# A fused encoder layer on one core: who issues the transfers of VectorE's turning of x, and when

## The reference

```python
h = rmsnorm(x, g_pre_mix) * (1 + scale1) + shift1
x = x + gate1 * rmsnorm(token_mixer(h, ...), g_post_mix)     # mLSTM heads | 2-D neighbourhood attention
h = rmsnorm(x, g_pre_ffn) * (1 + scale2) + shift2
x = x + gate2 * rmsnorm(expert_choice_moe(h, ...), g_post_ffn)   # 16 experts
```

## Time and profile before

| | us |
|---|---|
| median of 3 runs | 2347.81 (2345.64 to 2349.93) |
| the profiled execution | 2346.43 |
| its span, first to last instruction | 2344.6 |
| TensorE busy | 2238.1 (95%) |
| VectorE busy | 1410.6 (60%) |
| ScalarE busy | 1097.2 (47%) |
| GpSimd busy | 750.6 (32%) |
| mean granted TensorE clock | 0.987 |

### The profile page before, as it was taken

The page is one execution under the profiler, slowest core; times in us unless marked ns, Lnnn a source line. Parts: engine busy times, 40 slices in busy tenths (PEclk is TensorE's granted clock), DMA queues, the critical chain, the costliest instruction groups (busy, mean ns, idle before and its releaser), DMA issues. The chain is left out here.

```text
span 2344.6 us, 34389 instructions
## 1 busy us (share of the span) xinstructions
PE 2238.1 (95%) x13051; PEld 1861.2 (79%) x13051; DVE 1410.6 (60%) x2069; ACT 1097.2 (47%) x1768; POOL 750.6 (32%) x770
## 2 busy tenths in 40 slices
PE   6999999999999999999993999999999999999997
PEld 4679978977899888677772888888888888888886
DVE  3213354555413436665558777777778778888885
ACT  4213442555433435666542445444444445555553
POOL 3003332433233415341003422112222335443534
PEclk9999999999999999999996999999999999999998
DMA  8837785757554449764637576666666679999996
GB/s 317 268 112 231 220 231 170 220 147 190 140 186 153 153 157 245 213 202 142 203 130 273 215 248 229 225 218 225 226 225 228 225 260 310 312 320 322 320 302 230
DMA packets 234878, 524.06 MB, mean 224 GB/s; under 512 B 38964, under 2 KB 138180, under 8 KB 215280
## 3 DMA queue, kind: packets, MB, share of 16 engines
q1 hardware_dynamic: 185360, 407.37, 51.5%
q0 software_dynamic: 49376, 114.78, 17.7%
HBM read 423.71 MB, written 97.88 MB: 222 GB/s over the span
## 5 line engine op out<-in xcount | busy, mean ns | idle before, releaser
L2667 DVE TENSOR_TENSOR moe_w_lo<-moe_wf,moe_w_hi 128x2048 fp32r<-128x2048 f32 x192 | 436.7, 2287 | 196.1 <-ACT moe_w_hi L2523 195.1
L2523 ACT ACTIVATE moe_w_hi<-moe_wf 128x2048 fp32r<-128x2048 f32 x192 | 365.8, 1915 | 376.4 <-PE moe_acc L2853 362.2
L2853 PE MATMUL moe_acc<-moe_w_hi,moe_x_hi 128*128 128x512 f32 x1024 | 398.8, 389 | 0.9 <-DVE moe_x_lo L2673 0.6
L2853 PE MATMUL moe_acc<-moe_w_lo,moe_x_hi 128*128 128x512 f32 x1024 | 398.4, 389 | 0.0
L2853 PE MATMUL moe_acc<-moe_w_hi,moe_x_lo 128*128 128x512 f32 x1024 | 398.4, 389 | 0.0
L2853 PEld LDWEIGHTS moe_acc<-moe_w_hi,moe_x_hi 128*128 128x128 f32 x1024 | 192.2, 188 | 41.4 <-DVE moe_x_lo L2673 0.8
L2853 PEld LDWEIGHTS moe_acc<-moe_w_hi,moe_x_lo 128*128 128x128 f32 x1024 | 192.2, 188 | 40.1
L2853 PEld LDWEIGHTS moe_acc<-moe_w_lo,moe_x_hi 128*128 128x128 f32 x1024 | 192.2, 188 | 39.7
L2397 POOL DMA_INDIRECT moe_xe<-scratch_h,moe_parts x120 | 195.3, 1627 | 87.4 <-issue 76.2
L1874 PE MATMUL banks<-fr_w_hi,fr_h_hi 128*128 128x256 f32 x768 | 222.9, 290 | 0.0
L1874 PE MATMUL banks<-fr_w_lo,fr_h_hi 128*128 128x256 f32 x768 | 217.0, 283 | 0.0
(11 more groups left out here) (322 smaller groups left out, 4374.3 us busy)
## 6 DMA issues: line engine op xcount, KB each, us to landing
moe_wf<-in_w_expert_gate SPq DMA_DIRECT2D x64, 1024.0 KB, 5.7
moe_wf<-in_w_expert_up SPq DMA_DIRECT2D x64, 1024.0 KB, 5.1
moe_wf<-in_w_expert_down SPq DMA_DIRECT2D x64, 1024.0 KB, 6.9
fr_w_raw<-in_w_units SPq DMA_DIRECT2D x28, 1024.0 KB, 6.6
fr_bias<-in_na_bias SPq DMA_DIRECT2D x16, 1520.0 KB, 11.6
fr_a_w<-in_w_ada POOLq DMA_DIRECT2D x16, 1024.0 KB, 8.3
scratch_qk_t<-fr_stage SPq DMA_DIRECT2D x64, 256.0 KB, 2.7
scratch_vov<-fr_stage SPq DMA_DIRECT2D x96, 128.0 KB, 2.3
```

The lines of the kernel that those rows point to most:

```text
L2523: nc.scalar.activation(w_hi[:, q, :, :], wf[:, q, :, :], ACT.Copy).then_inc(w_hi_ready, 1)
L2667: nc.vector.tensor_tensor(w_lo[:, q, :, :], wf[:, q, :, :], w_hi[:, q, :, :].bitcast(F32), ALU.subtract).then_inc(w_lo_ready, 1)
L2853: mm = nc.tensor.matmul(acc[:, j, b, :], x[:, g, k, :], w[:, q, a, h * HALF:(h + 1) * HALF], start=(k == 0 and i == 0), stop=(k == KC - 1 ...
```

## The change

ScalarE issues the 16 loads and 16 stores of the four turning steps in place of SP. Loads are at tick 133 + 12 i, and the store of step i is at tick 145 + 12 i, just before the load of step i + 1; both stand behind `evac` and before `split_w` of their tick. VectorE's turns are at ticks 137 + 12 i and 138 + 12 i. The load of the turned quarter 2 moves from tick 184 to 192, its scaling from 196 to 204, and TensorE's spread of 1/rms for quarter 3 from 208 to 216.

```diff
@@ -165,10 +165,10 @@
 SQ_AT = {2: M1 - 30, 3: M1 - 26}
 TURN_AT = {1: 2 * TICKS + 3, 2: (M1 - 2) * TICKS, 3: (M1 + 2) * TICKS + 1}
 
-XQ_AT, XQ_STEP, XQ_STEPS = M1 - 25, 3, 4
-XT_AT = {2: M1 - 11, 3: M1}
-SPREAD_AT = {2: (M1 - 11) * TICKS, 3: (M1 - 5) * TICKS}
-SCALE_AT = {2: (M1 - 8) * TICKS, 3: (M1 + 2) * TICKS}
+XQ_AT, XQ_STEP, XQ_STEPS = M1 - 24, 3, 4
+XT_AT = {2: M1 - 9, 3: M1}
+SPREAD_AT = {2: (M1 - 11) * TICKS, 3: (M1 - 3) * TICKS}
+SCALE_AT = {2: (M1 - 6) * TICKS, 3: (M1 + 2) * TICKS}
 
 ROWS_AT = [(GATES_AT[g] + 2) * TICKS for g in range(GROUPS)]
 
@@ -501,19 +501,6 @@
                     sp.wait_ge(rows_stored, 64)
                 sp.dma_start(x[:, :, :], x_view[q]).then_inc(x_loaded, 16)
 
-            def load_xq(i):
-                if i:
-                    sp.wait_ge(xq_turned, FIRST_ADA + i)
-                else:
-                    sp.wait_ge(sq_ready, KC * 4)
-                for a in range(4):
-                    sp.dma_start(xa[32 * a:32 * a + 32, :, :], xq_view[XQ_STEPS + i, a]).then_inc(xq_loaded, 16)
-
-            def store_xq(i):
-                sp.wait_ge(xq_turned, FIRST_ADA + i + 1)
-                for a in range(4):
-                    sp.dma_start(xs_view[i, a], xb[32 * a:32 * a + 32, :, :]).then_inc(xq_stored, 16)
-
             def load_xt(q):
                 if q == 2:
                     sp.wait_ge(xq_stored, FIRST_ADA + 64 * XQ_STEPS)
@@ -618,11 +605,6 @@
                                 load_w(LOAD_AT[b])
                             if b in (SQ_AT[2] - 3, SQ_AT[3] - 3):
                                 load_x(2 if b < SQ_AT[2] else 3)
-                            step, late = divmod(b - XQ_AT, XQ_STEP)
-                            if late == 0 and 0 <= step < XQ_STEPS:
-                                load_xq(step)
-                            if late == 2 and 0 <= step < XQ_STEPS:
-                                store_xq(step)
                             if b in XT_AT.values():
                                 load_xt(2 if b < M1 else 3)
                             if b == NBLK - 12:
@@ -1084,6 +1066,19 @@
                     act.drain()
                     nc.scalar.activation(ps[:, PH, :], x[:, j, i * HALF:(i + 1) * HALF], ACT.Square, accum_out=ss[:, j, i:i + 1]).then_inc(sq_ready, 1)
 
+            def load_xq(i):
+                if i:
+                    act.wait_ge(xq_turned, FIRST_ADA + i)
+                else:
+                    act.wait_ge(sq_ready, KC * 4)
+                for a in range(4):
+                    act.dma_start(xa[32 * a:32 * a + 32, :, :], xq_view[XQ_STEPS + i, a]).then_inc(xq_loaded, 16)
+
+            def store_xq(i):
+                act.wait_ge(xq_turned, FIRST_ADA + i + 1)
+                for a in range(4):
+                    act.dma_start(xs_view[i, a], xb[32 * a:32 * a + 32, :, :]).then_inc(xq_stored, 16)
+
             def take_x(k):
                 act.wait_ge(turned, k + 1)
                 nc.scalar.activation(h_raw[:, k, 0:HALF], ps[:, k % 2, :], ACT.Copy).then_inc(xT_ready, 1)
@@ -1190,6 +1185,11 @@
                         if u == 0 and b >= 2:
                             for c in range(0 if b == 2 else b - 1, b):
                                 evac(c)
+                        step, late = divmod(b - XQ_AT, XQ_STEP)
+                        if (late, u) == (0, 1) and 0 < step <= XQ_STEPS:
+                            store_xq(step - 1)
+                        if (late, u) == (0, 1) and 0 <= step < XQ_STEPS:
+                            load_xq(step)
                         for q in (1, 2, 3):
                             if q > 1 and b == SQ_AT[q]:
                                 squares(q, u)
@@ -1552,8 +1552,8 @@
                 for b in range(NBLK):
                     for u in range(TICKS):
                         step, late = divmod(b - XQ_AT - 1, XQ_STEP)
-                        if late == 0 and 0 <= step < XQ_STEPS and u >= 2:
-                            turn_xq(step, u - 2)
+                        if late == 0 and 0 <= step < XQ_STEPS and u in (1, 2):
+                            turn_xq(step, u - 1)
                         for q in (1, 2, 3):
                             if q > 1 and (b, u) == (SQ_AT[q] + 1, 0):
                                 mean_of(q)
```

## The result

The changed kernel takes 2363.41 us (median of 4 runs, 2363.07 to 2366.13) where the kernel before, run beside it, took 2348.77: a ratio of 1.0067, interval 1.005 to 1.0084. It is slower by 0.67%, and the time lies above the forecast of 2351 and its range of 2341 to 2358. The profiled execution took 2363.07 us with a span of 2361.3, against 2346.43 and 2344.6, so its difference of 16.7 us in the span is the one to explain.

The account below looks back on a forecast made before the run. TensorE, busy 95% of the span, was taken as the bound, so only its idle time and clock count. Terms: +3.4 (tick 145, containing tick 133's -1.7) + 0 + 0 + 0 = +3.4 us, giving 2351; range 2341 to 2358.

Parts of the forecast that it names:

- Tick 133: First four loads on ScalarE: issues hidden in its idle time, the 1.73 us gap at qT goes, -1.7 us.
- Tick 145: Eight issues ahead of w_hi delay w_lo and `scores`; TensorE stands 5.0 us: +3.4 with clock, containing the earlier -1.7.
- Tick 157: Eight issues ahead of a weight piece; xa lands just in time for block 41's w_lo: 0, bounds -0.9 and +4.
- My sign for this tick: At tick 157: the forecast is wrong there if a gap over 1.5 us stands before L2072 near 325.
- Tick 169: Issues hide; the 3.78 us gap and 1.5 of clock go, a 3.3 to 5.3 us wait comes at turn_o: 0.
- Tick 181 and the scaling: Last four stores, and scaling moved into the last head's tail: 0, up to +1 for the scaling.
- Rival B: At tick 157, shared rings delay the next head's qT, a gap of 4 to 5 us: 2357 us; chance 0.32.
- Rival A: Issues are cheap on ScalarE, 3.1 us for eight; sum about -6, 2342 us; chance 0.24.

Follow-up runs that it names:

- Experiment 1: The changed kernel with its 32 issues back in SP's queue, at the new ticks; 2369.37 us, ratio 1.0095 against the kernel before.
- experiment 3: The changed kernel with ScalarE's weight piece of a tick ahead of that tick's issues; 2363.89 us, ratio 1.0076 against the kernel before.
- Experiment 5: The changed kernel with VectorE's turns 4 ticks later, from tick 141 + 12 i; 2354.94 us, ratio 1.0031 against the kernel before.
- experiment 7: The kernel before with only the turned x's load, the scaling and quarter 3's spread two blocks later; 2346.24 us, ratio 0.9997.
- experiment 2: The kernel before with ScalarE issuing the 32 transfers, at SP's old ticks; 2344.25 us, ratio 0.9985.
- experiment 10: The kernel before with only the 16 loads on ScalarE, at the old ticks, stores left on SP; 2342.09 us, ratio 0.9984.
- experiment 8: The kernel before, SP issuing, with turns at 137 + 12i and stores at 140 + 12i, ahead of the next load; 2351.44 us, ratio 1.0017.
- experiment 6: The changed kernel with turns 4 ticks later and ScalarE's weight piece ahead of its tick's issues; 2347.11 us, ratio 1.0002 against the kernel before.

## Why the prediction was wrong

**Tick 133: right in its term, with one oversight.** The qT gap went, -1.79 us against -1.7. The sentence that the next state is "due only at 284" took VectorE's wait for hidden. xa landed at 283.37, and the state came 1.18 us late. Experiment 1, with the load issued 5.5 us later still, makes 4.92 us of the same wait.

**Tick 145: right mechanism, undersized.** The chain of issues, w_hi, w_lo and `scores` is what stands in the trace, and experiment 3 takes the gap from 6.56 to 1.70 us by putting w_hi ahead. With the term of tick 133 I had +3.4; it measured +6.9. Eight issues took 7.4 us (3.1 and 4.31), not 6.2, and began later: w_hi started at 301.11 instead of 298.5. The gap was 6.56 us instead of 5.0, and the clock took 2.1 instead of 1.5.

**Tick 157 is the step that failed.** I put 0, with "landing takes 4.0 to 6.0 us" and "it just fits". Landing took 12.6 us behind the last issue. That issue ended 6.9 us later than I put it (331.09 against 324.2), but TensorE asked for block 41 6.7 us later too (339.70 against 333), so this cancels; the landing, 6.6 us over my upper value, and w_lo, 2.24 us against 1.2, make the gap. VectorE stood 9.19 us at the turn, block 41 started 7.43 us late, the clock cost 2.7, and the place measured +9.1 (from +6.87 to +15.96): more than half of the whole loss. Without it the time would have been near 2354, an estimate by the ledger, inside the range. My sign for this tick, a gap over 1.5 us before L2072 near 325, looked at the wrong consumer: there is no gap there, and the 7.43 us stand at block 41.

Two things were wrong in the term. The first is a reading. The 4.0 and 6.0 us are the minimum and median of single transfers, each from its own issue, but the turn waits for the last of four, and I left out the maximum of 9.5 in the same row. The kernel before shows the wait that counts: its first four were issued by 265.89 and the turn started at 273.08, 7.2 us later; its last four were issued by 338.88 and the turn started at 347.75, 8.9 us later.

```profile
273.08 1.25 DVE L1430 STREAM_TRANSPOSE fr_xb<-fr_xa 128x1024 f32<-128x1024 f32 x1 [6.22 <-DMA fr_xa<-in_x]
...
336.03 2.85 SPq L510 DMA_DIRECT2D fr_xa<-in_x  x4
```

With 8.9 the term would have been 324.2 + 8.9 + 1.25 + 1.2 = 335.6, some 2.6 us late and not 0. The second is the place: the rows of the kernel before come from loads at their old places. There the load of tick 152 was issued *ahead* of kT, qT and E, and the one of tick 157 now comes *behind* them, while they are moving. The rows by window say what it met there: the DMA engines' busy share in the changed kernel was 1.03 in 326 to 334 and 0.98 in 334 to 344, against 1.03 and 0.88 in the same windows before. A share near 1 alone does not set the two kernels apart; what differs is which transfers were ahead.

```profile
326.00:334.00 8.00, 8.00 (x45) 6.85 (x44) 1.34 (x3) 2.78 (x5) 2.52 (x2) 1.00 1.03 349
334.00:344.00 10.00, 5.70 (x34) 4.59 (x32) 0.74 (x3) 4.13 (x6) 2.65 (x2) 0.90 0.98 295
```

At the same time the change cut the distance between load and turn: from tick 128 to 134 before, from 133 to 137 now. A tick is some 2.1 us here (24 of them from the score at 302.09 to the one at 353.56), so 12.6 us became 8.4, of which the eight issues take about 7. Experiment 5 gives four ticks back and the turns' waits fall from 29.6 to 8.7 us.

**Tick 169: right.** The 3.78 us gap and its clock went (the ledger falls by 5.45, from +15.96 to +10.51), and 4.53 us with clock stands before turn_o; I had a wait of 3.3 to 5.3 us and a sum of 0, and it measured +0.9 (from +15.96 to +16.86). **Tick 181 and the scaling: right**, 0 by the ledger and by experiment 7.

**Rival B** had the side and nearly the size, but not the place. It let qT come late because two queues share the DMA engines; the gap at qT closed. What came late enough to be waited for was xa. Other transfers of SP did slow down, as it said: at tick 157 the next head's v landed 11.4 us after its issue and the first E 12.9, against 9.1 and 9.0 before. With a single ring, in experiment 1, the third xa landed no sooner after kT's issue (21.2 us against 20.6), so this lateness can come without a second ring; whether the ring shares in it where there are two, no run tells apart. **Rival A** (cheap issues, 3.1 us for eight) is refuted by the 6.8 to 7.4 us that eight took. But its sign was right for the half of the change that it is about: at the old places, experiment 2, ScalarE's issues did pay.

What stays open: whether xa was late because its packets waited behind those of the next head, or because each of those transfers slowed all others. Both give a late landing under load; that at tick 157 even the first of the four landed 11.6 us after its issue fits either. No run here took the next head's loads away. Nor was a kernel run with tick 157 alone at its old place.

## What to carry to other kernels

When a load is moved, take its landing time, that of the last transfer of the group, from what else is in flight at the new place and not from its own rows at the old one, and count the ticks from the load to its consumer again. A consumer that waits in an in-order queue makes everything behind it late, so putting single instructions ahead of it only moves the gap, and two late causes at one place must be taken away together before the gain of either shows there. An issue costs its engine half a microsecond to one: give an idle engine's queue the loads that must start early, and leave stores where nothing waits behind them.

## What the runs showed of the hardware

- The price of an issue depends on what was queued just before. A load issue on ScalarE took 472 ns in the median when it stood alone (322 to 569, experiment 2), and 848 ns in the changed kernel (403 to 1906), where three of the four groups stand right behind four stores. These three groups took 3.54 to 4.31 us for four, the first, without stores ahead, 2.56.
- The same megabyte, in four transfers, landed 5.4 us after its last issue at tick 169 and 12.6 and 13.2 us beside the next head's loads. In experiment 1 the delay lay in SP's queue instead: it began the third four 10 us behind kT, took 5.33 us to issue them, and they landed 5.9 us later (341.73 to 347.65).
- TensorE's clock fell from 2.4 to 1.2 GHz for a part of the time behind standstills of 4.53, 6.56 and 7.43 us, which cost 1.7, 2.1 and 2.7 us beside the gaps; it stayed at 2.4 GHz behind 2.14 us (experiment 10) and 1.39 us (kernel before). Shorter standstills than these three cost clock too: the mean granted clock was 0.77 in 362 to 368 of experiment 8 (2.73 us), 0.76 in 354 to 360 of experiment 2 (3.06 us) and 0.76 in 356 to 362 of experiment 6 (3.15 us).
